# Fourier transform over tokens folded twice instead of once, the last attention combination on four piece buffers, and one weight load moved ahead in the dilated attention's queue

## The chip, the cores and the metric

One core of a Trainium2 chip runs one program. The metric is the device time of that program in microseconds (us); a shorter time is better. All arithmetic is in float32.

## The reference, cut to what matters

Two blocks run one after the other on 2048 tokens of width 1024. The change touches only the second. From its normalised input it projects a part `u_f` (512 wide) for a Fourier mixer, gates, and queries, keys and values for dilated window attention with three dilations, whose outputs are combined with softmax weights `alpha`.

```python
u_f = u_f.reshape(B, S, N_FOURIER_GROUPS, HEAD_DIM)
f = jnp.fft.fft2(u_f, axes=(1, 3), norm="ortho").real.astype(jnp.float32)
f = jnp.einsum('bsgc,gcd->bsgd', f, w_fourier.astype(jnp.float32)).reshape(B, S, FOURIER_WIDTH)
y_f = f * jax.nn.silu(g_f)
...
alpha = jax.nn.softmax(jnp.stack(lses, axis=0), axis=0)
o = jnp.sum(alpha[..., None] * jnp.stack(outs, axis=0), axis=0).reshape(B, S, ATTN_WIDTH)
y_a = o * jax.nn.silu(g_a)
mixed = jnp.concatenate([y_f, y_a], axis=-1) @ w_out.astype(jnp.float32)
h = h + mixed
```

The Fourier part runs over the 2048 tokens (the axis of the change) and over 64 channels of a group. Both are done as matrix products with tables of cosines and sines.

## The kernel before

The program is a row of blocks; in each, every engine has its own list of instructions, and they wait for each other on semaphores. At a block's end all engines meet. Matrix products on TensorE (PE) take four passes' worth of time per column in float32 and appear in the trace as two instructions (two passes over the columns) each.

**Dilated attention** (`dilated_attention`). Four groups g of 128 channels; in each, five steps n project two column blocks of the weights with seven products in place of eight (`SevenProducts`, `project`). A step needs four quarters of weights in `raw` (loads 0 to 3, `SevenProducts.load`, issued by SyncE, SP) and four differences `mixed` made by GpSimd (POOL, `SevenProducts.make`, L2353 to L2362). Product 2 of a step needs the second difference (L2356), which needs quarter 3. From g = 1 on, the step n = 5g also combines the attention outputs of group g - 1: the tokens are cut into eight pieces of 256; for each, SP fetches two stored outputs, the gate and the broadcast weights `alpha` (`fetch_piece`, L2511, L2512, L2519), POOL does five operations (`combine`, L2571 to L2578), and SP stores the result (`keep_piece`, L2529). A piece's fetch waits until the piece two before is combined, since there are two piece buffers.

**The Fourier block** (`fourier`). The combination of the last group is done here, beside the Fourier projections. The projections are ND = 2 rounds d of four units f (f = 4d to 4d + 3), seven products each (L3612) in the order 1, 2, 4, 6, 5, 7, 3; `HALVES` says which half of the tokens a unit takes. Units 4d and 4d + 1 make `us[0]` and `us[1]` (two channel groups of u), units 4d + 2 and 4d + 3 make their gates in `mix`. Products rotate over four PSUM banks; ScalarE (ACT) holds products 1 and 4 (`hold`, into `x` and `y`), VectorE (DVE) adds the others (`add`, L3768), POOL does two joins (`join`, L3554, L3557). The gates of round 0 lie in rows 2 and 3 of `mix_f`, where the two piece buffers are too, so `add` and `join` of unit 2 wait for all eight combined pieces (L3551, L3766).

After each round come two transforms over tokens, g = 2d and 2d + 1. DVE folds token t with token 2048 - t (`fold`, L3779 to L3783) into sums and differences of 1024 each; PE multiplies these by 128 x 128 channel matrices (L3638, 16 products of 128 columns), ACT copies the results to `co` (L3701), PE treats the middle token apart (L3643, L3646, L3647, L3656) and does 16 products of 512 columns with the table `trig` (L3654), of which 4 MB is fetched anew for each transform. ACT collects two of four result banks (`collect`, L3325), DVE joins them to 2048 tokens (`join`, L3335 to L3345) and multiplies by the gate (L3791).

**The output projection** (`project_second`) follows, 224 products at L2205. The last transform's join and gate product are done in it, and it needs four weight combinations that DVE makes (`FourierTail.make`, L3313 to L3318) from `w_out`.

Of the kernel before, what the change touches and what calls it, by code (L numbers as in the profile page):

```python
# [2077 lines left out]
def project_second(nc, t, mix_f, mix_att, hT, w, late, tail):  # L2078
# [6 lines left out]
    with ExitStack() as ctx:  # L2085
# [26 lines left out]
        def bank_of(j, i):  # L2112
            return (5 + ORDER.index((j, i))) % 8

        with nc.Block() as block:
# [99 lines left out]
            @block.scalar  # L2215
            def _(act):
                tail.collect(nc, act, bank, PAIRS - 1)
                for j in range(NJ):
                    act.wait_ge(prod, done(j, 1))
                    need(act, held, 7 * (j - 4) + 4)  # L2220
                    nc.scalar.copy(m1[:, j % 4], bank[bank_of(j, 1)][:]).then_inc(m1_out, 1)

            @block.vector
            def _(dve):
# [24 lines left out]
                tail.join(nc, dve, bank, PAIRS - 1)  # L2249
# [35 lines left out]
class SevenProducts:  # L2285
# [61 lines left out]
    def make(self, nc, pool, n):  # L2347
# [8 lines left out]
        nc.gpsimd.tensor_tensor(mixed[:, 1], raw[:, 3], mixed[:, 0], ALU.subtract).then_inc(self.made, 1)  # L2356
        need(pool, self.prod, done + 5)
# [96 lines left out]
class Combine:  # L2454
# [6 lines left out]
    def __init__(self, nc, ctx, sems):  # L2461
# [4 lines left out]
        piece = [self.rows[:, 2 + i, 0:6 * self.NQ].rearrange("p (m n) -> p m n", n=self.NQ) for i in range(2)]  # L2466
        self.alpha = [p[:, 0:3] for p in piece]
        self.others = [p[:, 3:5] for p in piece]
        self.gate = [p[:, 5] for p in piece]
# [11 lines left out]
        self.piece_in = [sem("c_piece_in0"), sem("c_piece_in1")]  # L2481
        self.weighed = sem("c_weighed")
# [4 lines left out]
        self.wo_in = [sem(f"c_wo{k}") for k in range(KC)]  # L2487

# [16 lines left out]
    def fetch_rows(self, sp, t, g, m):  # L2505

        NQ, i = self.NQ, m % 2
        cols = slice(m * NQ, (m + 1) * NQ)
        if m >= 2:
            sp.wait_ge(self.mixed, self.PIECES * g + m - 1)  # L2510
        sp.dma_start(self.others[i], t["o_rows"][g].rearrange("c p n -> p c n")[:, :, cols]).then_inc(self.piece_in[i], 16)  # L2511
        sp.dma_start(self.gate[i], t["g_rows"][g][:, cols]).then_inc(self.piece_in[i], 16)  # L2512

    def fetch_alpha(self, sp, t, g, m):

        half, NQ, i = P // 2, self.NQ, m % 2
        for h in range(2):
            rows = slice(h * half, (h + 1) * half)
            sp.dma_start(self.alpha[i][rows], t["alpha"][g, :, h, m * NQ:(m + 1) * NQ].partition_broadcast(half)).then_inc(self.piece_in[i], 16)  # L2519
# [44 lines left out]
    def combine(self, nc, pool, g, m, dst=None):  # L2564

        i = m % 2
        n = self.PIECES * g + m
        alpha, others, gate = self.alpha[i], self.others[i], self.gate[i]
        own = self.o[:, m * self.NQ:(m + 1) * self.NQ]
        pool.wait_ge(self.piece_in[i], 64 * (n // 2 + 1))  # L2570
# [10 lines left out]
def dilated_attention(nc, t, seven, late):  # L2581
# [33 lines left out]
    with ExitStack() as ctx:  # L2615
# [64 lines left out]
        with nc.Block() as block:  # L2680
            @block.sync
            def _(sp):
# [54 lines left out]
                for g in range(PAIRS):  # L2737
# [8 lines left out]
                    else:  # L2746
# [57 lines left out]
            def _(pool):  # L2804
# [12 lines left out]
                seven.make(nc, pool, 0)  # L2817
# [7 lines left out]
                for n in range(5 * PAIRS):  # L2825
                    g, p = divmod(n, 5)
                    mixing = g > 0 and p < 2
                    for j in range(2):
# [9 lines left out]
                        if mixing and p == 0:  # L2838
                            if j == 0:
                                late.weights_pool(nc, pool, g - 1)  # L2840
                            else:
                                pool.wait_ge(out, NB * N_CFG * g)
                                late.combine(nc, pool, g - 1, 0)
                                late.combine(nc, pool, g - 1, 1)
# [6 lines left out]
                    seven.make(nc, pool, n + 1)  # L2851
# [431 lines left out]
class FourierTail:  # L3283
# [4 lines left out]
    def __init__(self, nc, ctx, hT, room, sems):  # L3288
# [4 lines left out]
        self.ue = room[:, 5].rearrange("p (i n) -> p i n", i=2)  # L3293
        self.s = self.ue[:, :, :].rearrange("p i n -> p (i n)").rearrange("p (s n) -> p s n", n=M // 2)
        self.qs = sb("qs5", [P, 2, M // 2])
        self.mid_out = sb("mid_out5", [P, 1])
# [23 lines left out]
    def collect(self, nc, act, bank, g):  # L3320
# [3 lines left out]
        for i in range(2):  # L3324
            nc.scalar.copy(self.qs[:, i], bank[2 * i + 1][:]).then_inc(self.qs_out, 1)  # L3325
        nc.scalar.copy(self.mid_out[:], bank[4][:, 0:1]).then_inc(self.qs_out, 1)

    def join(self, nc, dve, bank, g):
# [3 lines left out]
        f, s, qs, mid_out, joined = self.us[g % 2], self.s, self.qs, self.mid_out, self.joined  # L3332
        dve.wait_ge(self.qs_out, 3 * g + 3)
        for i in range(2):
            nc.vector.tensor_tensor(s[:, 2 * i], bank[2 * i][:], qs[:, i], ALU.add).then_inc(joined, 1)  # L3335
# [591 lines left out]
```

## Time and profile before

| | us |
|---|---|
| time, median of 3 runs (3505.53 to 3507.4) | 3505.95 |
| time of the profiled execution | 3506.91 |
| span of the profile (first to last instruction) | 3504.9 |
| PE busy | 3353.2 (96%) |
| DVE, ACT, POOL busy | 1284.6, 1017.1, 918.6 |
| mean granted TensorE clock | 0.986 |

The span is the time from the first to the last instruction in the profile; what the run's time has beyond it (2.0 us here) lies around the program. The profiled execution is 0.96 us above the median. In the rows below, "x8" of a PE line counts instructions, two to a product; the number before a line's engine is its duration, the one before that its start, both in us.

### The profile page before, as it was taken

What the parts mean: (1) busy time and instruction counts of PE and PEld (TensorE: products, weight loads), DVE (VectorE), ACT (ScalarE), POOL (GpSimd) and SP (SyncE); (2) the same over time, 40 slices, a digit from 0 to 9 for tenths busy, and PEclk for the clock granted to TensorE, in tenths of its full rate; (3) what the DMA queues carried; (4) which work ended last, traced back from release to release, by engine and by line L of the source; (5) the groups of instructions that cost most, each with busy time, mean ns of one, the idle gap of its engine ahead of it and who ended that gap; (6) DMA issues with size and microseconds to landing.
All of it is one profiled execution on the core that took longest, in us unless ns stands there. A gap on an engine that the chain in (4) does not pass through costs nothing. (4 is left out here: it accounts for less than half of the span.)

```text
span 3504.9 us, 43834 instructions
## 1 busy us (share of the span) xinstructions
PE 3353.2 (96%) x16395; PEld 1818.3 (52%) x16395; DVE 1284.6 (37%) x2780; ACT 1017.1 (29%) x2411; POOL 918.6 (26%) x705
## 2 busy tenths in 40 slices
PE   8999999998999999998999999999999999889999
PEld 4485858583545445443544554445454545444444
DVE  3344352534424434444323432333243324423422
ACT  4313131331414323332323422442243224110100
POOL 1002020206253352534211241124112321421132
PEclk9999999999999999999999999999999999999999
DMA  7101010113021123221167154725372726331421
GB/s 229 28 20 36 20 37 13 32 59 84 17 51 28 37 46 134 90 96 48 31 34 49 44 90 37 49 56 75 40 46 58 75 44 38 87 117 53 192 96 60
DMA packets 284381, 217.11 MB, mean 62 GB/s; under 512 B 124604, under 2 KB 249932, under 8 KB 278752
## 3 DMA queue, kind: packets, MB, share of 16 engines
q1 hardware_dynamic: 281068, 214.30, 31.4%
q8 instruction: 132, 2.16, 0.3%
q14 instruction: 77, 0.63, 0.1%
q10 hardware_dynamic: 3104, 0.01, 0.1%
HBM read 168.47 MB, written 45.81 MB: 61 GB/s over the span
## 5 line engine op out<-in xcount | busy, mean ns | idle before, releaser
L2406 PE MATMUL d<-hT,w_tiles 128*128 128x512 f32 x1280 | 579.4, 596 | 5.2 <-DMA w_tiles<-in_w_in 5.2
L2406 PE MATMUL d<-w_room,w_tiles 128*128 128x512 f32 x960 | 440.8, 602 | 17.3 <-POOL w_tiles L2356 17.3
L2406 PEld LDWEIGHTS d<-hT,w_tiles 128*128 128x128 f32 x1280 | 242.4, 191 | 303.9 <-issue 296.8
L549 PE MATMUL m<-hT,w 128*128 128x512 f32 x704 | 321.1, 593 | 1.3 <-ACT pre L699 1.3
L2406 PEld LDWEIGHTS d<-w_room,w_tiles 128*128 128x128 f32 x960 | 182.8, 193 | 243.4 <-issue 220.9
L2443 POOL TENSOR_TENSOR w_z<-w_u,w_y 128x512 f32<-128x512 f32 x40 | 50.7, 1268 | 814.5 <-ACT w_y L2412 814.5
L1364 PE MATMUL n<-hT,wo 128*128 128x512 f32 x512 | 226.5, 597 | 4.8 <-DMA wo<-in_w_in 4.8
L549 PEld LDWEIGHTS m<-hT,w 128*128 128x128 f32 x704 | 124.9, 191 | 116.0 <-issue 115.8
L1364 PE MATMUL n<-mix_na,wo 128*128 128x512 f32 x384 | 169.4, 594 | 0.9 <-POOL wo L1264 0.9
L3056 ACT ACTIVATE mix_f<-sneg,negmax 128x192 f32<-128x192 f32 (+1 forms) x384 | 161.0, 426 | 5.6 <-DVE negmax L3170 5.6
L1364 PEld LDWEIGHTS n<-hT,wo 128*128 128x128 f32 x512 | 96.7, 191 | 125.6 <-issue 120.0
L497 POOL TENSOR_TENSOR hn<-hn 128x512 f32<-128x512 f32 x16 | 17.5, 1094 | 544.3 <-DVE hn L866 544.3
L563 PEld LDWEIGHTS m<-w,hT 128*128 128x128 f32 x1280 | 143.6, 192 | 2.4 <-issue 1.4
L563 PE MATMUL m<-w,hT 128*128 128x128 f32 x1280 | 143.9, 275 | 0.8 <-DVE v L815 0.8
L3612 PE MATMUL f<-hT,w_tiles 128*128 128x512 f32 x256 | 115.4, 607 | 13.0 <-DVE mix_f L3768 8.8
L1364 PEld LDWEIGHTS n<-mix_na,wo 128*128 128x128 f32 x384 | 71.7, 190 | 87.7 <-issue 85.3
L3170 DVE CUSTOM_DVE_ANT_0 sneg<-d,bias 128x192 f32<-128x192 f32 (+1 forms) x384 | 108.3, 324 | 23.4 <-PE d L2901 14.6
L2867 PE MATMUL d<-sq,ones 128*128 128x512 f32 x192 | 98.8, 596 | 4.2 <-ACT sq L3022 4.2
L2435 DVE TENSOR_TENSOR w_u<-d,w_u 128x512 f32<-128x512 f32 x64 | 44.3, 692 | 147.7 <-PE d L2406 147.7
L3027 ACT ACTIVATE rt<-d,eps 128x512 f32<-128x512 f32 x96 | 66.0, 688 | 108.2 <-PE d L2867 108.2
L2915 PE MATMUL d<-ident,mix_f 128*128 128x128 f32 x600 | 85.9, 280 | 9.0 <-ACT mix_f L3056 7.5
L3612 PE MATMUL f<-w_room,w_tiles 128*128 128x512 f32 x192 | 85.8, 604 | 8.1 <-POOL w_tiles L3541 8.1
(389 smaller groups left out, 5230.3 us busy)
## 6 DMA issues: line engine op xcount, KB each, us to landing
w_tiles<-in_w_in SPq DMA_DIRECT2D x96, 256.0 KB, 3.1
trig<-in_trig SPq DMA_DIRECT2D x16, 1024.0 KB, 4.9
mix_f<-alpha SPq DMA_DIRECT2D x64, 192.0 KB, 6.4
ada<-in_w_ada SPq DMA_DIRECT2D x8, 1024.0 KB, 11.5
xg<-in_x SPq DMA_DIRECT2D x4, 2048.0 KB, 16.2
w<-in_w_in SPq DMA_DIRECT2D x16, 512.0 KB, 3.9
rb<-r_rows SPq DMA_DIRECT2D x16, 512.0 KB, 4.9
wo<-in_w_in SPq DMA_DIRECT2D x32, 256.0 KB, 3.4
```

The costliest lines, as they stand in the source:

```text
L549: last = nc.tensor.matmul(bank[n % 2][:], w[:, k], hT[:, k, (n % 4) * TB:(n % 4 + 1) * TB], start=(k == 0), stop=(k == KC - 1))
L563: last = nc.tensor.matmul(bank[n % 2][:, j * P:(j + 1) * P], hT[:, k, c * P:(c + 1) * P], w[:, k], start=(k == 0), stop=(k == KC - 1))
L1364: last = nc.tensor.matmul(bank_of(f, i)[:], w[:, k], xs[k], start=(k == 0), stop=(k == h - 1))
L2406: last = nc.tensor.matmul(bank[self.bank_of(n, j, i)][:], w[:, k], x[k], start=(k == 0), stop=(k == h - 1))
L2435: nc.vector.tensor_tensor(dst, bank[self.bank_of(n, j, i)][:], other, ALU.add).then_inc(self.full, 1)
L2443: nc.gpsimd.tensor_tensor(self.z[:], u, self.y[:], ALU.add).then_inc(self.pooled, 1)
L2867: nc.tensor.matmul(bank[S_BANK][:], ones[:], sq[:, e % 2], start=True, stop=True).then_inc(ssq, 1)
L2915: last = nc.tensor.transpose(bank[T_BANK + j][:, i * P:(i + 1) * P], prob[:, u % (2 * BU), part_ * P:(part_ + 1) * P], ident[:])
L3027: nc.scalar.activation(rt[:, e % 2], bank[S_BANK][:], ACT.Ln, bias=epst[:, 0:1], scale=1.0 / half).then_inc(rooted, 1)
L3056: nc.scalar.activation(prob[:, u % (2 * BU), off:off + n], sneg[:, (U * a + u) % 6, 0:n], ACT.Exp, bias=negmax[:, c, u:u + 1], scale=-1.0, ...
L3170: nc.vector.tensor_tensor_reduce(out=sneg[:, (U * a + u) % 6, 0:n], in0=bank[b][:, c0:c0 + n], in1=bias[:, i % 2, c, t0:t0 + n], scale=1.0 ...
L3612: last = nc.tensor.matmul(bank_of(f, i)[:], w[:, k], xs[k], start=(k == 0), stop=(k == h - 1))
```

## The change

Three things change.

- **Dilated attention**: SP issues load 3 of step 5g + 1 before piece 2 and not after it; `make` is cut in two, and POOL combines piece 1 between the halves and not before both.
- **Last combination**: its pieces use four buffers that lie in the memory of `trig` and `co` (not yet in use then). So SP can fetch four pieces at once, and `add` and `join` of unit 2 no longer wait for it. The softmax factors come earlier in the lists of DVE, ACT and POOL. The makes of the next weights are interleaved otherwise with the pieces.
- **Transform**: the tokens are folded twice. `fold` first adds and subtracts token t and t + 1024, then folds each half, in place in `us`; the table is a quarter in size (2 MB, fetched once, after the last combined piece). The 16 products with it have 256 columns. There are two sets of four banks, so the channel products of transform 2d + 1 are issued between the products of transform 2d, and the middle tokens of both in one go (`middles`). `fold(2d + 1)` moves before unit 4d + 3's adds, and `FourierTail.make` before `finish(2)`.

```diff
     def fetch_rows(self, sp, t, g, m):
-        NQ, i = self.NQ, m % 2
+        NQ = self.NQ
+        landed, _, others, gate = self.piece(g, m)
+        depth = 4 if g == PAIRS - 1 else 2
         cols = slice(m * NQ, (m + 1) * NQ)
-        if m >= 2:
-            sp.wait_ge(self.mixed, self.PIECES * g + m - 1)
+        if m >= depth:
+            sp.wait_ge(self.mixed, self.PIECES * g + m - depth + 1)
...
                         load(n + 1, 2)
                         fetch_bias(g)
+                        load(n + 1, 3)
                         late.fetch_piece(sp, t, g - 1, 2)
                         late.keep_piece(sp, t, g - 1, 0)
-                        load(n + 1, 3)
...
-                    seven.make(nc, pool, n + 1)
+                    seven.make_first(nc, pool, n + 1)
+                    if mixing and p == 0:
+                        late.combine(nc, pool, g - 1, 1)
+                    seven.make_last(nc, pool, n + 1)
...
-        trig = sb("trig5", [P, NTR, 4, H])
+        trig = sb("trig5", [P, NK, 4, 2, Q])
-        co = sb("co5", [P, 2, MC, P])
+        co = sb("co5", [P, 2, 4, 2, NK, P])
+        late.wide = [trig[:, i].rearrange("p n e j -> p (n e j)") for i in range(2)] + [co[:, e].rearrange("p s r k c -> p (s r k c)") for e in range(2)]
...
+                def fetch_trig(k):
+                    sp.wait_ge(late.mixed, late.PIECES * PAIRS)
+                    sp.dma_start(trig[:, k], t["trig"][k]).then_inc(trig_in, 16)
...
+                for m in range(2):
+                    late.fetch_piece(sp, t, LAST, m + 4)
+                    late.keep_piece(sp, t, LAST, m)
                 load(N0 + 1, 0)
+                late.fetch_piece(sp, t, LAST, 6)
+                late.keep_piece(sp, t, LAST, 2)
+                late.fetch_piece(sp, t, LAST, 7)
+                late.keep_piece(sp, t, LAST, 3)
                 load(N0 + 1, 3)
...
-                sp.wait_ge(prod, 7 * 4 * ND)
+                sp.wait_ge(prod, product_no(4 * ND - 1, 5))
+                for k in range(PAIRS, KC):
+                    fetch_out(k)
                 for k in range(PAIRS):
                     fetch_out(k)
...
-                        elif d == 0:
-                            pool.wait_ge(late.mixed, late.PIECES * PAIRS)
...
+                def coefficients(g):
...
+                    for i in range(2):
+                        pe.wait_ge(folded, 12 * g + 7 + 5 * i)
+                        for r in range(2):
+                            for m in range(4):
+                                c = 4 * (2 * i + r) + m
+                                last = nc.tensor.matmul(second_banks[2 * i + r][:, m * P:(m + 1) * P], us[e][:, c * P:(c + 1) * P], ab[:, e, i], start=True, stop=True)
+                        last.then_inc(coef, 1)
+                def middles(d):
+                    pe.wait_ge(full, 5 * 4 * (d + 1))
+                    pe.wait_ge(pooled, 2 * 4 * (d + 1))
+                    pe.wait_ge(folded, 12 * (2 * d + 1) + 12)
+                    for e in range(2):
+                        last = nc.tensor.matmul(first_banks[3][0:1, e * P:(e + 1) * P], us[e][:, M:M + 1], ab[:, e, 0], start=True, stop=True)
+                    last.then_inc(mids, 1)
+                def transform(g, n):
...
+                    for odd in range(2):
+                        for k in range(NK):
+                            stop = k == NK - 1 and not (n == 0 and odd == 0)
+                            last = nc.tensor.matmul(dst[:, odd * Q:(odd + 1) * Q], co[:, e, 2 * i + odd, r, k], trig[:, k, n, odd], start=(k == 0), stop=stop)
+                        if n == 0 and odd == 0:
+                            pe.wait_ge(mids_out, d + 1)
...
                 def fold(g):
...
+                    nc.vector.tensor_tensor(p, u[:, 0:M], u[:, M:T], ALU.add).then_inc(folded, 1)
+                    nc.vector.tensor_tensor(q, u[:, 0:M], u[:, M:T], ALU.subtract).then_inc(folded, 1)
+                    dve.wait_ge(folded, 12 * g + 2)
+                    for s0 in (0, 2):
+                        for s, src in ((s0, p), (s0 + 1, q)):
+                            op = ALU.add if s in (0, 3) else ALU.subtract
+                            nc.vector.tensor_tensor(part[:, s, 0, 1:Q], src[:, 2:H:2], src[:, M - 2:H:-2], op).then_inc(folded, 1)
+                            nc.vector.tensor_tensor(part[:, s, 1], src[:, 1:H:2], src[:, M - 1:H:-2], op).then_inc(folded, 1)
+                        nc.vector.tensor_copy(singles(s0), of_both(0 if s0 == 0 else H)).then_inc(folded, 1)
```

The first place is one transform on PE, the pair after round 0 (a row is a group of products; `f0` to `f7` are the PSUM banks, `mid5` the middle token's row). Before, it stands so:

```order
L3643 MATMUL f0<-ab5,w_room 1x128
L3646 MATMUL f0<-alt_row5,mid5 128x512
L3647 MATMUL f4<-one5,mid5 128x1
L3654 MATMUL f0<-trig5,co5 128x512
L3654 MATMUL f1<-trig5,co5 128x512
L3654 MATMUL f2<-trig5,co5 128x512
L3654 MATMUL f3<-trig5,co5 128x512
L3656 MATMUL f4<-alt_col,co5 128x1
```

Of the change, the same place and what follows up to transform 1's first bank:

```order
L3658 MATMUL f3<-ab5,w_room 1x128 x2
L3674 MATMUL f0<-trig5,co5 128x256 x2
L3677 MATMUL f0<-alt_row5,mid5 128x256
L3674 MATMUL f0<-trig5,co5 128x256 x2
L3674 MATMUL f1<-trig5,co5 128x256 x4
L3687 MATMUL f3<-alt_col,co5 128x1 x2
L3688 MATMUL f3<-one5,mid5 128x1
L3649 MATMUL f4<-ab5,w_room 128x128 x4
L3649 MATMUL f5<-ab5,w_room 128x128 x4
L3649 MATMUL f6<-ab5,w_room 128x128 x4
L3649 MATMUL f7<-ab5,w_room 128x128 x4
L3674 MATMUL f2<-trig5,co5 128x256 x4
```

The table products went from 512 to 256 columns at the same number, the middle row's product came behind two of them, and the next transform's channel products (L3649) stand in the middle.

The second place is SP's queue in the dilated attention, g = 1, from the bias fetch on (`w_tiles` is the weight quarter, the rest are pieces). Before:

```order
L2693 DMA bias<-in_alibi 64x576 x2
L2511 DMA mix_f<-o_rows 128x2x256
L2512 DMA mix_f<-g_rows 128x256
L2519 DMA mix_f<-alpha 64x3x256 x2
L2529 DMA att_rows<-mix_f 128x256
L2345 DMA w_tiles<-in_w_in 128x4x128
```

And of the change:

```order
L2708 DMA bias<-in_alibi 64x576 x2
L2345 DMA w_tiles<-in_w_in 128x4x128
L2526 DMA mix_f<-o_rows 128x2x256
L2527 DMA mix_f<-g_rows 128x256
L2535 DMA mix_f<-alpha 64x3x256 x2
L2545 DMA att_rows<-mix_f 128x256
```

The quarter moved past a fetch that waits for piece 0 and a store that does too.

The third place is POOL in the Fourier block, from the third combined piece to the fifth (`L2586` is the first of a piece's five operations, `L3565` and `L3568` the joins of a unit, `L3554` a weight difference). Of the change:

```order
L2593 TENSOR_TENSOR mix_f<-mix_f,co 128x256
L3565 TENSOR_TENSOR w_room<-u,qs 128x512
L2586 TENSOR_TENSOR co<-co 128x512
L2587 TENSOR_TENSOR mix_f<-mix_f,co 128x256
L2589 TENSOR_TENSOR mix_f<-mix_f,co 128x256
L2591 TENSOR_TENSOR mix_f<-mix_f,co 128x256
L2593 TENSOR_TENSOR mix_f<-mix_f,co 128x256
L3554 TENSOR_TENSOR w_tiles<-w_tiles 128x512
L3568 TENSOR_TENSOR w_room<-u,qs 128x512
L2586 TENSOR_TENSOR trig<-trig 128x512
```

Pieces lie in `co` and `trig` in place of `mix_f`, and the first weight difference stands ahead of the join and not behind it; all eight pieces still stand ahead of unit 2's first join.

## Rows read from the trace of the kernel before

**Rows 1.** Whom PE waited for: us in total, times, longest.

```profile
PE d L2406 <- POOL w_tiles L2356: 17.3, 4, 5.7
PE f L3612 <- DVE mix_f L3768: 8.8, 1, 8.8
PE f L3612 <- POOL w_tiles L3541: 8.1, 1, 8.1
PE f L3612 <- DVE w_room L3768: 3.0, 1, 3.0
```

**Rows 2.** Timeline of PE, dilated attention: a product undisturbed, then three after a wait.

```profile
2003.61 3.60 PE L2406 MATMUL d<-w_room,w_tiles 128*128 128x512 f32 x8
2021.62 6.01 PE L2406 MATMUL d<-w_room,w_tiles 128*128 128x512 f32 x8 [4.97 <-POOL w_tiles L2356]
2365.63 6.38 PE L2406 MATMUL d<-w_room,w_tiles 128*128 128x512 f32 x8 [5.74 <-POOL w_tiles L2356]
2709.25 5.24 PE L2406 MATMUL d<-w_room,w_tiles 128*128 128x512 f32 x8 [5.02 <-POOL w_tiles L2356]
```

**Rows 3.** Timeline of SP and POOL at the first of these places.

```profile
2013.21 0.39 SPq L2345 DMA_DIRECT2D w_tiles<-in_w_in  x1
2020.30 1.26 POOL L2356 TENSOR_TENSOR w_tiles<-w_tiles 128x512 f32<-128x512 f32 x1 [2.74 <-DMA w_tiles<-in_w_in]
2010.20 2.17 POOL L2571 TENSOR_TENSOR mix_f<-mix_f 128x512 f32<-128x512 f32 x1
```

**Rows 4.** Timeline of PE: ends of rounds 0 and 1, the output's start.

```profile
2990.91 3.67 PE L3612 MATMUL f<-hT,w_tiles 128*128 128x512 f32 x8 [1.23 <-PEq L76]
3103.55 10.46 PE L3612 MATMUL f<-hT,w_tiles 128*128 128x512 f32 x24
3162.16 3.68 PE L3612 MATMUL f<-hT,w_tiles 128*128 128x512 f32 x8
3248.97 10.46 PE L3612 MATMUL f<-hT,w_tiles 128*128 128x512 f32 x24
3307.11 10.54 PE L2205 MATMUL f<-hT,w_room 128*128 128x512 f32 x24 [1.14 <-PEq L76]
```

**Rows 5.** Timeline of SP and POOL in round 0.

```profile
3011.45 1.28 SPq L2502 DMA_DIRECT2D alpha<-part  x3
3002.22 2.68 POOL L3554 TENSOR_TENSOR w_room<-u,qs 128x512 f32<-128x512 f32 x1 [11.01 <-ACT qs L3684]
3020.84 1.27 POOL L2571 TENSOR_TENSOR mix_f<-mix_f 128x512 f32<-128x512 f32 x1 [9.41 <-DMA mix_f<-alpha]
3025.16 1.26 POOL L2571 TENSOR_TENSOR mix_f<-mix_f 128x512 f32<-128x512 f32 x1
3086.09 1.26 POOL L3554 TENSOR_TENSOR mix_f<-u,qs 128x512 f32<-128x512 f32 x1 [0.17 <-POOL mix_f L2578]
```

**Rows 6.** DMA issues from 3033 to 3046 us: KB each, median us to landing.

```profile
w_tiles<-in_w_in SPq DMA_DIRECT2D x2, 256.0 KB, 8.5
```

**Rows 7.** Timeline of PE in the first transform.

```profile
3114.79 3.84 PE L3638 MATMUL f<-ab,w_room 128*128 128x128 f32 x32 [0.78 <-DVE mix_f L3768]
3126.33 0.28 PE L3656 MATMUL f<-alt_col,co 128*128 128x1 f32 x2
3126.47 3.68 PE L3654 MATMUL f<-trig,co 128*128 128x512 f32 x8
3129.99 0.28 PE L3656 MATMUL f<-alt_col,co 128*128 128x1 f32 x2
```

**Rows 8.** Timeline of PE in the first block: a product of 258 columns and its successor.

```profile
453.39 0.60 PE L605 MATMUL m<-state,qT 128*128 128x258 f32 x2
453.85 0.71 PE L611 MATMUL m<-v,sd 128*128 128x129 f32 x4
```

**Rows 9.** Timeline of DVE: a join's first operation and its gate product.

```profile
3163.51 0.69 DVE L3335 TENSOR_TENSOR w_room<-f,qs 128x512 f32<-128x512 f32 x1 [14.61 <-ACT mid_out L3326]
3168.81 2.29 DVE L3791 TENSOR_TENSOR mix_f<-w_room,mix_f 128x2048 f32<-128x2048 f32 x1
```

More of the change, by code:

```diff
@@ L2465, in __init__ @@
         self.o = self.rows[:, 1]
[L2466 to L2469, printed above, removed]
+        self.near = [self.rows[:, 2 + i] for i in range(2)]
+        self.wide = None
         self.stat = sb("stat6", [P, 2, N_CFG, U])
@@ L3463, in _ @@
                 late.fetch_stats(sp, t, LAST)
-                late.fetch_rows(sp, t, LAST, 0)
-                late.fetch_rows(sp, t, LAST, 1)
+                for m in range(4):
+                    late.fetch_rows(sp, t, LAST, m)
+                load(N0 + 1, 1)
+                late.store_alpha(sp, t, LAST)
+                for m in range(4):
+                    late.fetch_alpha(sp, t, LAST, m)
                 sp.wait_ge(once, 2)
@@ L3568, in _ @@
                 late.combine(nc, pool, LAST, 3)
+                make(N0 + 1, 1)
                 join(1, 2)
[L3570 removed]
                 late.combine(nc, pool, LAST, 4)
[L3572 to L3574 removed]
+                make(N0 + 1, 2)
+                make(N0 + 1, 3)
+                late.combine(nc, pool, LAST, 5)
+                make(N0 + 1, 4)
+                for m in range(6, late.PIECES):
                     late.combine(nc, pool, LAST, m)
@@ L3617, in weigh_channels @@
                         pe.wait_ge(consts, 48)
+                    else:
+                        pe.wait_ge(joined, 12 * (2 * d - 1) + 4)
                     pe.wait_ge(wd_in, 64 * (d + 1))
-                    need(pe, qs_out, 3 * 2 * d)
                     for e in range(2):
                         for i in range(2):
-                            last = nc.tensor.matmul(bank[3][:, (2 * e + i) * P:(2 * e + i + 1) * P], chan[:, i], wd[:, e], start=True, stop=True)
+                            last = nc.tensor.matmul(second_banks[3][:, (2 * e + i) * P:(2 * e + i + 1) * P], chan[:, i], wd[:, e], start=True, stop=True)
@@ L3633, in transform @@
                     for i in range(2):
-                        pe.wait_ge(folded, 6 * g + 4 + 2 * i)
-                        for m in range(MC):
-                            if e == 1 and i == 1 and m == 4:
-                                pe.wait_ge(qs_out, 3 * g)
-                            last = nc.tensor.matmul(bank[BANKS[2 * i + m // 4]][:, (m % 4) * P:(m % 4 + 1) * P], ue[:, i, m * P:(m + 1) * P], ab[:, e, i], start=True, stop=True)
-                        last.then_inc(coef, 1)
-                    if g > 0:
-                        pe.wait_ge(qs_out, 3 * g)
-                        pe.wait_ge(joined, 12 * (g - 1) + 4)
@@ new lines, in transform @@
+                def transform(g, n):
+                    d, e = divmod(g, 2)
+                    i, r = divmod(n, 2)
+                    dst = tail.banks(g)[n]
+                    pe.wait_ge(co_out, 4 * g + 2 + 2 * i)
+                    if g == 0 and n == 0:
+                        pe.wait_ge(trig_in, 16 * NK)
+                    if n == 3:
+                        pe.wait_ge(centre_out, g + 1)
+                    for odd in range(2):
+                        for k in range(NK):
+                            stop = k == NK - 1 and not (n == 0 and odd == 0)
+                            last = nc.tensor.matmul(dst[:, odd * Q:(odd + 1) * Q], co[:, e, 2 * i + odd, r, k], trig[:, k, n, odd], start=(k == 0), stop=stop)
+                        if n == 0 and odd == 0:
+                            pe.wait_ge(mids_out, d + 1)
+                            nc.tensor.matmul(dst[:, 0:Q].rearrange("p (n c) -> p n c", c=P), mid[0:1, e], alt_row[:, :].unsqueeze(1).broadcast_to([1, Q // P, P]), start=False, stop=True)
+                    if n == 3:
+                        last.then_inc(done, 1)
@@ L3659, in _, with output_centre @@
+                def output_centre(g):
+                    d, e = divmod(g, 2)
+                    dst = tail.banks(g)[3][:, H - 1:H]
+                    pe.wait_ge(co_out, 4 * g + 4)
+                    for k in range(NK):
+                        nc.tensor.matmul(dst, co[:, e, 0, 0, k], alt_col[:], start=(k == 0), stop=False)
+                    nc.tensor.matmul(dst, mid[0:1, e], one[0:1, :], start=False, stop=True).then_inc(centre, 1)
                 for d in range(ND):
```

265 lines of the change are left out of this document (119 added, 146 removed).

## The prediction

> **What bounds the kernel now.** I read the shares of busy time first: TensorE (PE) works 96% of the span, so time is won only where PE has less to do or stops waiting. So I asked next whom PE waits for [rows 1]. Four entries touch this change: 17.3 us for the weight difference of L2356 in the dilated attention, and 8.8, 8.1 and 3.0 us in the Fourier block. Then the timeline of PE at each. In the dilated attention there are three long waits, one in each of the groups 1 to 3: 4.97, 5.74 and 5.02 us, 15.73 together (the fourth of the 17.3 is at the stage's start and stays). The same rows show a second loss: the eight passes behind a wait take 6.01, 6.38 and 5.24 us, where 3.60 is the undisturbed figure [rows 2], 6.83 us more in all. PE's clock is at its lower level (1.2 GHz, half of 2.4) behind such a stop.
>
> In the Fourier block, rounds 0 and 1 are the same work on PE. Round 0 runs from 2990.91 to 3114.01 (3103.55 + 10.46), 123.10 us; round 1 from 3162.16 to 3259.43, 97.27 us [rows 4]. So round 0 loses 25.83 us; 19.9 of it are the three waits [rows 1], 5.9 the clock behind them. The transforms take 48.15 us after round 0 (3114.01 to 3162.16) and 47.68 us after round 1 (3259.43 to 3307.11, change of block included) [rows 4]. I work with these four stretches.
>
> **Part 1, the weight quarter in the dilated attention.** POOL starts L2356 at 2020.30, released by the DMA of quarter 3, which SP issued at 2013.21 [rows 3] behind a fetch and a store that wait for the first piece. The load's own condition is product 6 of the half step before, whose passes start at 2003.61 [rows 2] and are over at about 2007.1. So it goes out 6 us earlier, and no piece's transfers are ahead of it. POOL now makes the two differences before piece 1, which starts at 2010.20 today [rows 3]. If the quarter still takes 7.1 us to land (2013.21 to 2020.30), the second difference is done at 2015.5; if POOL's list sets it, at 2012.8. PE wants it at 2016.65 (2021.62 less its wait). Cover 1.1 to 3.8 us; I take the whole 15.73 + 6.83 = 22.6 us.
>
> What is late next: piece 1 and the last two differences now stand between PE's earlier start and the next unit's first join. At 4.32 us a piece (3020.84 to 3025.16, [rows 5]) and one wait for a fetch, that join comes some 4 us after its input. It holds up the addition of product 5, whose bank PE wants back three products later; over 6 us are left. I leave 1 us of loss: **-21.6 us**. Bounds: 17 (the quarter late by 1 us each time, with part of the clock loss) to 22.6.
>
> **Part 2, round 0.** POOL's list is the clock here. Today the first join starts at 3002.22, `alpha` goes out at 3011.45, the first piece is combined from 3020.84, and unit 2's first join starts at 3086.09, behind all eight pieces [rows 5]; PE's 8.8 us wait is for the addition behind it. In the changed order the factors no longer wait for the first join but for DVE's three sums (over at about 2997.8), so I put store and first piece 6 us earlier: 3014.8. From there eight pieces are 34.6 us, two joins and four differences of 1.2 to 1.3 us are 7.5: 3056.9 with no wait. Two things are added.
> - Quarter 3 of the next weights goes out behind piece 3 and the fetch of piece 7, at about 3036.5. Loads in this stretch took 8.5 us to land [rows 6]; I take 7.5, so the second difference is made at about 3046.7. PE, if it never stops, wants it for its sixteenth product: 15 at 3.44 us (97.27 less 0.9 for the channel weights, by 28 products) and that 0.9 are 3043.4. **A wait of 3.3 us, and 1.7 us of clock behind it**, a little under a third of 6.83.
> - An operation of DVE on two tensors in SBUF holds POOL up: 2.68 us beside one [rows 5] for what takes 1.26 alone [rows 3]. Fold 0 and two changes of sums fall into POOL's pieces: 3 to 6 us.
>
> So unit 2's join is done at 3063 to 3067. With the stop above, PE wants its bank at about 3069; without it at 3064. No second stop, then. Of 25.8 us, 5.0 stay: **-20.8 us**. Bounds: no stop (-25.8), and 12 us (-13.8: the difference 5 us late, the join 3 us, each with 2 us of clock).
>
> The Trainium skill (SBUF — State Buffer, "Who interferes with whom") says that VectorE and GpSimd hold their shared port pair as an exclusive lock. The trace agrees in kind (2.68 against 1.26 us). By the rule fold 0 (some 5 us) and both changes (2.3 us each) would be POOL's loss in full, and the join would be done at about 3068.
>
> **Part 3, the transforms.** Per transform the channel products stay, 32 passes of 128 columns in 3.8 us. The table products stay 16 in number, 32 passes; eight of 512 columns take 3.52 us (3126.47 to 3129.99), 0.44 each [rows 7]. A pass of 256 columns doesn't stand in the trace; the nearest has 258, two in 0.46 us (453.39 to 453.85, [rows 8]), weight loads among them, and 0.22 is half of 0.44. Between 0.22 and 0.23 I take 0.22: 7.0 us (14.1 before). The middle row's product is 0.44, the centre column three products of 0.14 (3126.33 to 3126.47, [rows 7]), the middle token 0.24. A transform is 3.8 + 7.04 + 0.44 + 0.42 + 0.24 = 11.94 us, two are 23.9. Waits: the middle row is wanted some 5.1 us in, and ACT is through with four copies and the row some 5.4 us in: 0.3 us. Today's waits go: 0.78 us at the start [rows 7], since the channel products don't wait for the last addition, and those for the join of the transform before, since the two have banks of their own. Pair 0: 24.2 in place of 48.15, **-24.0 us**.
>
> Pair 1 ends with a change of block, where all engines meet, and there DVE sets the end. Transform 2 is done 16.2 us into the pair, ACT has copied two banks by 17.5, join and gate product take 7.6 us (3163.51 to 3168.81 + 2.29, [rows 9]): 25.1, and 1.14 us for the change of block [rows 4]: 26.3 in place of 47.68, **-21.4 us**. `FourierTail.make`, four operations of 2.29 us, stands ahead of this join. `w_out` is asked for two products (6.9 us) before the pair begins; if it is there 8 us into it, `make` is done in time, and what is later goes to the end one for one. I allow 2 us.
>
> Folding costs DVE more, some 5 us in place of 2.8 by the columns, and fold 1 or 3 runs ahead of the last unit's additions. DVE is free for 6 us there (one more product's time less an addition), and behind it PE has three more banks, 10 us: nothing. The join now writes every second column; I price that as today, at the worst 1.5 us more.
>
> **Sum.** -21.6 - 20.8 - 24.0 - 21.4 = -87.8. The profiled execution took 3506.91, so 3419.1; the median lies 0.96 below it: **3418 us**.
>
> **Rivals.**
> 1. *The four terms hold*, with 0 to 8 us lost in round 0 (chance 0.70): 3411 to 3424.
> 2. *Round 0's stall moves instead of going* (0.14). POOL still has all eight pieces ahead of unit 2's join, and four pieces of `alpha` share the queues with the weight quarter. For it: the 8.5 us landing; against it: 2 to 6 us of cover for the join. With 9 us or more of stops: 3423 to 3432.
> 3. *The shorter passes don't take half* (0.07). If something other than the columns set a pass's time (its weight load, say) and it stayed at 0.44, 128 passes would cost 28 us more: 3446; half of that loss is 3432. Against it: the two passes of 258 columns, which have loads too. The Trainium skill (TensorE: Matmul & The Clock Gate, "The mechanism") says that loads overlap running matmuls only in another row group; by it this would be the case. The measured 0.46 us doesn't agree.
> 4. *No stop in round 0 and DVE off the end* (0.06): 3408 to 3411.
> 5. *The change doesn't do what it says* (0.02): the load isn't what PE waits for, and the rounds' waits reappear; it would need three terms to fail.
> 6. *Slower than before* (0.01): PE's clock stays at the lower level through the short passes. That costs as much again as the work done under it; both pairs are 48 us, and it decides from 88 us of work on, so it would have to last 40 us into the rounds. Against it: the clock came back inside eight passes after each stop [rows 2].
>
> **Range.** 3408 to 3434. Down: 5.0 (no stop), 1.0 (part 1's rest), 1.1 (DVE off the end), 2 to 3 for the spread of runs and of my starts. Up: 7 (12 us of stops), 4.6 (part 1 at its low bound), 3.4 (one fall of the clock in each pair), 1. About 0.2% (7 us) is what a measurement of this kernel can tell from no change. Faster by more than that 0.97, within it 0.02, slower 0.01.
>
> **What the profile after would show.** Part 1: no wait of PE over 1 us for the second difference in groups 1 to 3, and the next join later behind its input. Part 2: round 0 of 97 to 105 us, one wait of some 3 us at product 2 of unit 2, for POOL's weight difference, and none for DVE's addition in unit 2. Part 3: passes of 256 columns 0.22 us apart, pairs of about 24 and 26 us, PE's last block released by DVE's gate product. The prediction is wrong if PE waits over 5 us at unit 3's first products, if the passes are 0.3 us or more apart, or if `w_out` holds up the end.

## The result, and the profile after

The median went from 3505.74 us (3505.16 to 3507.4, 4 runs) to **3426.16 us** (3422.98 to 3429.14, 4 runs): ratio 0.9771, 95% interval [0.9756, 0.9786]. The prediction was 3418 (3408 to 3434). The profiled execution took 3427.26 us with a span of 3425.4, against 3506.91 and 3504.9: 79.65 us less where the sum had 87.8. Each term can be read off TensorE's (PE's) timeline. Here are the starts that answer to [rows 4]:

```profile
2977.63 3.67 PE L3622 MATMUL f<-hT,w_tiles 128*128 128x512 f32 x8 [1.24 <-PEq L76]
...
3032.84 12.26 PE L3622 MATMUL f<-w_room,w_tiles 128*128 128x512 f32 x24 [2.58 <-POOL w_tiles L3554]
...
3068.98 10.46 PE L3622 MATMUL f<-hT,w_tiles 128*128 128x512 f32 x24
3079.28 3.73 PE L3649 MATMUL f<-ab,w_room 128*128 128x128 f32 x32
...
3092.26 4.48 PE L3674 MATMUL f<-trig,co 128*128 128x256 f32 x20
...
3104.29 1.02 PE L3622 MATMUL f<-hT,w_tiles 128*128 128x512 f32 x2
...
3199.60 1.88 PE L3622 MATMUL f<-hT,w_tiles 128*128 128x512 f32 x4
...
3227.59 2.81 PE L2205 MATMUL f<-hT,w_room 128*128 128x512 f32 x6 [1.10 <-PEq L76]
```

A row is start, duration, instruction, and in brackets how long PE had stood still and for whom. Taking each stretch from these starts, and that of before from [rows 4]:

| stretch | before | after | difference | forecast |
|---|---|---|---|---|
| all ahead of the Fourier block | 2990.91 | 2977.63 | -13.3 | -21.6 |
| round 0 | 123.10 | 101.81 | -21.3 | -20.8 |
| transforms, pair 0 | 48.15 | 24.85 | -23.3 | -24.0 |
| round 1 | 97.27 | 97.19 | -0.1 | 0 |
| transforms, pair 1, with the change of block | 47.68 | 26.11 | -21.6 | -21.4 |

Round 0 ends at 3068.98 + 10.46 = 3079.44, round 1 at 3199.60 + 1.88 = 3201.48. Three terms are right to 0.7 us, and the first is short by 8.3, about what the sum as a whole is short by (8.15). Of its 13.3 us, 1.15 lie ahead of the first scores of the dilated attention (1929.63 before, 1928.48 after), in code that is the same in both; from there to the Fourier block it is 12.1. Yet the waits that it counted are gone. What PE waited for after (whom, us in total, times, longest), with one entry of ScalarE (ACT) that the kernel before doesn't have:

```profile
PE d L2919 <- issue: 12.8, 8, 3.4
PE d L2412 <- DMA w_tiles<-in_w_in: 5.3, 1, 5.3
PE d L2412 <- POOL w_tiles L2357: 2.6, 1, 2.6
ACT w_y L2418 <- DMA v_rows<-w_y: 42.9, 3, 14.9
```

Of the four waits for the second weight difference in [rows 1] only that at the stage's start is left. At the place of [rows 3] the quarter now leaves at 2006.12, the difference is made at 2011.31 with no wait, and PE's product starts at 2015.32. But the first line, PE's scores, was 7.2 us with a longest of 0.9 before. The new stop is at the end of the value projections of groups 1 to 3. Timeline after: the load and the difference just named, PE, then the engines behind the new stop in the order in which they release each other:

```profile
2006.12 0.38 SPq L2345 DMA_DIRECT2D w_tiles<-in_w_in  x1
2011.31 1.27 POOL L2357 TENSOR_TENSOR w_tiles<-w_tiles 128x512 f32<-128x512 f32 x1
2015.32 3.60 PE L2412 MATMUL d<-w_room,w_tiles 128*128 128x512 f32 x8
...
2056.52 3.60 PE L2412 MATMUL d<-hT,w_tiles 128*128 128x512 f32 x8
2063.49 1.15 PE L2919 MATMUL d<-kT,mix_f 64*64 64x128 f32 x16 [3.37 <-issue]
2064.56 1.98 PE L2900 MATMUL d<-ident,pt 128*128 128x128 f32 x8
...
2402.80 1.56 PE L2919 MATMUL d<-kT,mix_f 64*64 64x128 f32 x16 [3.09 <-issue]
...
2741.90 0.88 PE L2919 MATMUL d<-kT,mix_f 64*64 64x128 f32 x16 [1.88 <-issue]
...
2044.18 0.38 SPq L2526 DMA_DIRECT2D mix_f<-o_rows  x1
2047.51 0.43 SPq L2740 DMA_DIRECT2D v_rows<-w_y  x1
...
2055.10 0.59 ACT L2418 COPY w_y<-d 128x512 f32<-128x512 f32 x1 [14.91 <-DMA v_rows<-w_y]
2055.86 1.27 POOL L2449 TENSOR_TENSOR w_z<-w_u,w_y 128x512 f32<-128x512 f32 x1 [4.99 <-DMA v_rows<-w_z]
2057.16 0.69 DVE L2441 TENSOR_TENSOR w_u<-d,w_u 128x512 f32<-128x512 f32 x1 [9.98 <-POOL w_z L2449]
2057.08 1.27 POOL L2586 TENSOR_TENSOR mix_f<-mix_f 128x512 f32<-128x512 f32 x1
2061.40 1.26 POOL L2452 TENSOR_TENSOR w_y<-w_u,w_y 128x512 f32<-128x512 f32 x1
2062.69 0.69 DVE L2441 TENSOR_TENSOR pt<-d,w_u 128x512 f32<-128x512 f32 x1 [4.25 <-POOL w_y L2452]
```

SyncE (SP) fetches piece 7 at 2044.18, when piece 5 is combined, and issues the store of the first value block (`w_y`, `w_z`) only behind that, at 2047.51. The store, behind the piece's transfers, takes 7.6 us to land. ACT needs `w_y` for the next half step and copies into it at 2055.10. GpSimd's (POOL's) join and VectorE's (DVE's) addition follow. Then POOL combines piece 7, 4.3 us that stand between its two joins in the kernel before as well; its second join starts at 2061.40, and DVE's last addition is over at 2063.38. The scores start 0.1 us later. In the kernel before the same places read:

```profile
2049.46 1.19 SPq L2725 DMA_DIRECT2D v_rows<-w_y  x1
...
2058.63 0.59 ACT L2412 COPY w_y<-d 128x512 f32<-128x512 f32 x1 [9.71 <-PE d L2406]
...
2069.73 0.88 PE L2901 MATMUL d<-kT,mix_f 64*64 64x128 f32 x16 [0.90 <-issue]
```

There the store left at 2049.46 and ACT came for `w_y` 9.2 us later, released by PE. After the change PE is 8.7 us further at this place (its last projection ends at 2060.12 in place of 2068.84), but the store is only 1.95 us earlier, because the pieces keep their own pace. ACT would have come for `w_y` 8.7 us earlier too, at 2049.9, and gets it at 2055.10, 5.2 us late. Of these, 2.5 us reach PE as the longer stop (3.37 for 0.90); the scores and transposes behind it then run partly at the lower clock (1.98 for eight transposes that take 1.24 undisturbed, section 2; the granted clock is 0.58 from 2063.49 to 2066.50, and 0.50 behind the stop at 2402.80).

### The profile page after: what moved, and what is told of

It reads as the page before. It is cut to its first block and busy times, and to the rows that moved or that the text cites. A ratio compares the mean times of both kernels' runs of the same rounds, so it can differ in the third digit from the quotient of the medians.

```text
span 3425.4 us, 43810 instructions
## 1 busy us (share of the span) xinstructions
PE 3307.9 (97%) x16379; PEld 1812.2 (53%) x16379; DVE 1299.9 (38%) x2804; ACT 1016.2 (30%) x2409; POOL 923.5 (27%) x705
## 5 line engine op out<-in xcount | busy, mean ns | idle before, releaser
L2919 PE MATMUL d<-kT,mix_f 64*64 64x192 f32 (+1 forms) x1536 | 80.2, 319 | 17.7 <-issue 12.8
## 6 DMA issues: line engine op xcount, KB each, us to landing
ada<-in_w_ada SPq DMA_DIRECT2D x8, 1024.0 KB, 11.6
```

Of the source, the lines that this page charges most:

```text
L2919: last = nc.tensor.matmul(bank[b][dst, c0:c0 + n], q[src, u * half:(u + 1) * half], kT[src, k0:k0 + n], start=True, stop=True)
```

## The experiments

All ratios are to runs of the kernel before on the same chip.

### 1. Each part alone

The dilated part alone in the kernel before is the diff's load, `make_first` and `make_last`, nothing of the Fourier block. The Fourier part alone is the kernel after with these lines undone:

```diff
                         fetch_bias(g)
-                        load(n + 1, 3)
                         late.fetch_piece(sp, t, g - 1, 2)
                         late.keep_piece(sp, t, g - 1, 0)
+                        load(n + 1, 3)
...
                                 late.combine(nc, pool, g - 1, 0)
+                                late.combine(nc, pool, g - 1, 1)
...
                     seven.make_first(nc, pool, n + 1)
-                    if mixing and p == 0:
-                        late.combine(nc, pool, g - 1, 1)
                     seven.make_last(nc, pool, n + 1)
```

> The kernel before with the dilated part alone (the quarter's load ahead of piece 2 and the weight differences split around piece 1). The sum of the prediction, with nothing late behind the stop: -21.6 us, so 3484 us against 3505.7. Theory A (the stop moves: the store of the first value block leaves SyncE's queue too late, ScalarE's copy into w_y waits for it, and the scores start 2.5, 2.2 and 1.0 us later, with 1.4 to 2.5 us of clock behind each): -12 us, 3493.7 us, and in the trace ScalarE waits for v_rows<-w_y by some 40 us in all as in the kernel after. Rival B (the shortfall is made by the two parts together, not by this one): 3484 us and no such waits.

> The kernel after with the dilated part undone. The two parts share no engine time, so by the prediction's terms -20.8 - 24.0 - 21.4 = -66.2 us, 3439.5 us; by the trace of after (-21.3, -23.3, -21.6) 3439.5 us too. If the missing 8 us came from the Fourier block, it would be 3447 us.

Measured: 3493.23 us for the dilated part, ratio 0.9964 [0.9951, 0.9976], and 3439.9 us for the Fourier part, 0.9812 [0.9798, 0.9825]. Both medians are within 0.5 us of what was expected, the first of them by theory A; that run's five times spread over 10 us (3487.94 to 3497.84), so that close an agreement is partly luck, but theory A's 12 and rival B's 21.6 us are well apart. The dilated part alone leaves the same wait of ACT and the same stop behind it:

```profile
ACT w_y L2418 <- DMA v_rows<-w_y: 44.6, 3, 15.0
PE d L2910 <- issue: 14.4, 8, 3.5
```

So the shortfall belongs to the dilated part by itself, and the parts add up: -12.3 and -65.7 are -78.0, against -79.6 for both.

### 2. The store ahead of piece 7

```diff
                         late.keep_piece(sp, t, g - 1, 4)
+                        store_block(n + 1, 0, t["v_rows"][g])
                         late.fetch_piece(sp, t, g - 1, 7)
                         late.keep_piece(sp, t, g - 1, 5)
-                        store_block(n + 1, 0, t["v_rows"][g])
```

It was made on the kernel after, on the kernel before with the dilated part, and on the kernel before by itself.

> The kernel after with the stores of the first value block issued ahead of the fetch of piece 7 instead of behind it. Theory A: ScalarE's copy into w_y waits for no store, the scores start 0.9 us behind the last projection again, and 5.6 us of stops and 4 to 5 us of clock go: 3415 to 3417 us. Rival C (what makes the scores late is VectorPool work itself, GpSimd's joins standing behind the pieces, whose pace is set by their fetches of 6.4 us each): no change, 3426 us, the same stops of 3.4 us, and ScalarE's copy no earlier to any use.

> The kernel before with the dilated part and the first value block's stores ahead of piece 7. Theory A (the store alone stood between the dilated part and its full worth): 3484 us, the -21.6 us of the prediction's first term, with no wait of ScalarE for v_rows<-w_y. Rival (some of the 21.6 was never there): the -12.3 of the part alone less the 9.9 that the store brought in the whole kernel gives no less than 3483, so anything above 3487 would speak for it.

> The kernel before with nothing but the first value block's stores ahead of piece 7. ScalarE's copy waited for no store there, so by theory A nothing changes: 3506 us, within 2. Rival (the early store is worth 10 us by itself, whatever the dilated part does): 3496 us.

Measured, in this order: 3416.25 us (0.9745 [0.9731, 0.9758]); 3484.48 us (0.9937 [0.9924, 0.9949]); 3506.27 us (0.9997 [0.9988, 1.0005]). In the kernel after the moved store leaves at 2039.77, ACT waits for PE alone, and the stop is gone with the slow passes behind it:

```profile
2039.77 0.43 SPq L2740 DMA_DIRECT2D v_rows<-w_y  x1
...
2049.12 0.58 ACT L2418 COPY w_y<-d 128x512 f32<-128x512 f32 x1 [9.71 <-PE d L2412]
...
2060.23 0.88 PE L2919 MATMUL d<-kT,mix_f 64*64 64x128 f32 x16 [0.90 <-issue]
2061.04 1.24 PE L2900 MATMUL d<-ident,pt 128*128 128x128 f32 x8
```

The three together settle it. The same edit is worth 9.9 us behind the dilated part and nothing before it, and the dilated part with it is worth 3505.7 - 3484.5 = 21.2 us (to 3507.53, the median of its own chip, 23.1), where the forecast had 21.6. The traces say it more sharply. From the first scores of group 0 to the Fourier block it is 1061.28 us before, 1049.15 after, and 1038.14 and 1038.17 in the two kernels with the dilated part and the early store: 23.1 us less than before, 11.0 less than after. (In the second of the two, PE's wait for a weight difference in round 0 is 10.3 us where it was 8.1, which is what its whole time has less.) Rival C (POOL's joins behind the pieces) falls: POOL's order of work is the same here, piece 7 between the joins included, and the stop is gone.

### 3. Half the dilated part

One run moves the load and leaves all four differences behind piece 1, another splits the differences and leaves the load.

> The kernel after without the split of the weight differences: the quarter's load is ahead of piece 2, but piece 1 is combined ahead of all four differences. GpSimd's piece of 4.33 us then stands in front of the second difference, which ended at 2012.6 in the kernel after and would end at 2016.9, against a product that wants it at about 2015.5 in its trace: a stop of 1 to 2 us and 1.5 us of clock, three times, while the late store and the stop ahead of the scores stay: 3432 to 3436 us. Rival: the load alone did it, and the split is worth nothing: 3426 us.

> The kernel after with the quarter's load where it was, behind the store of piece 0, and the differences split around piece 1. The load leaves at about 2012 and lands 7 us later, as in the kernel before, and GpSimd now waits for it with piece 1 behind it: a stop of some 5 us as in the kernel before stays, three times, and the pieces come later too, so that the stop ahead of the scores grows: 3450 us or more, up to that of the Fourier part alone (3440) plus 15. Rival: the split alone is enough: 3426 us.

Measured: 3427.04 us (0.9773 [0.976, 0.9787]) without the split, 3439.56 us (0.9807 [0.9794, 0.9821]) without the load. Both expectations were too high, for one reason. The first number is that of the rival (the split is worth nothing), but not for its reason, that PE would not stop. Without the split PE does stop for the second difference, as expected, but the stop at the scores is then gone:

```profile
2017.73 5.40 PE L2412 MATMUL d<-w_room,w_tiles 128*128 128x512 f32 x8 [2.36 <-POOL w_tiles L2357]
...
2065.22 0.88 PE L2918 MATMUL d<-kT,mix_f 64*64 64x128 f32 x16 [0.90 <-issue]
```

PE loses 2.36 us and 1.80 of clock (5.40 for 3.60) at the first place, and no longer arrives too early at the second. In groups 2 and 3 it stops as long, but the passes behind take 3.70 us: the same stop costs the clock in one group and not in the others. I had added the two stops; they take each other's place, and with the late store the split is worth nothing that can be told. Without the load ahead the stops for the difference are 4.62, 5.25 and 4.38 us, one longer stop at the scores is left (2.09, group 2), and the time is that of the Fourier part alone. If that is so, the split must be worth something once the store is early, which the last run of the next section tests.

### 4. Round 0: its one stop, and the one behind it

The stop of 2.58 us was in the forecast: POOL has the second difference at 3031.52, since quarter 3 leaves SP at 3024.84. The next kernel (with the early store) issues quarter 0 one piece earlier and quarter 3 two (not one, as the expectation below has it), and makes the second difference ahead of piece 4. The one after it also puts unit 2's first join ahead of piece 7:

```diff
-                for m in range(2):
-                    late.fetch_piece(sp, t, LAST, m + 4)
-                    late.keep_piece(sp, t, LAST, m)
+                late.fetch_piece(sp, t, LAST, 4)
+                late.keep_piece(sp, t, LAST, 0)
                 load(N0 + 1, 0)
+                late.fetch_piece(sp, t, LAST, 5)
+                late.keep_piece(sp, t, LAST, 1)
+                load(N0 + 1, 3)
                 late.fetch_piece(sp, t, LAST, 6)
                 late.keep_piece(sp, t, LAST, 2)
                 late.fetch_piece(sp, t, LAST, 7)
                 late.keep_piece(sp, t, LAST, 3)
-                load(N0 + 1, 3)
...
                 join(1, 2)
+                make(N0 + 1, 2)
                 late.combine(nc, pool, LAST, 4)
-                make(N0 + 1, 2)
...
                 make(N0 + 1, 4)
-                for m in range(6, late.PIECES):
-                    late.combine(nc, pool, LAST, m)
+                late.combine(nc, pool, LAST, 6)
+                join(2, 1)
+                late.combine(nc, pool, LAST, 7)
                 for f in range(2, 4 * ND):
-                    join(f, 1)
+                    if f > 2:
+                        join(f, 1)
```

> The kernel of the store moved ahead, and in the first round of the Fourier block the loads of weight quarters 0 and 3 one fetched piece earlier each, with the second weight difference ahead of the fifth combined piece. TensorE's only stop of that round (2.58 us, for the second difference, and 1.8 us of clock behind it) should go: 4.4 us below the run of the store alone, 3411 to 3413 us. Rival: the joined rows of unit 2, which stand behind the pieces on GpSimd and were done at 75 us of the round, become the stop, and the gain is under 2 us.

> The kernel of the run before (store and quarters ahead), with the first join of unit 2 in the Fourier block ahead of the last combined piece on GpSimd. There the stop had only moved: TensorE waited 2.76 us for VectorE's addition to unit 2's rows, which stood behind GpSimd's join at 3039.28. Theory D (the join stands behind the pieces, and is ready to run after the seventh): the join runs 4.3 us earlier, the round has no stop and no fall of the clock, and 4.4 us go: 3410 us (3409 to 3411). Rival: VectorE's own fold in front of that addition sets it, and the time stays at 3414.

Measured: 3414.44 us (0.9738 [0.9725, 0.9751]) and then 3411.45 us (0.9731 [0.9718, 0.9745]). In the first of them the rival won. PE's stop for the weight difference is gone, and the join, still behind all eight pieces, takes its place:

```profile
3041.39 5.27 PE L3623 MATMUL f<-hT,w_tiles 128*128 128x512 f32 x8 [2.76 <-DVE mix_f L3820]
...
3038.60 0.72 POOL L2593 TENSOR_TENSOR mix_f<-mix_f,co 128x256 f32<-128x256 f32 x1
3039.28 1.26 POOL L3566 TENSOR_TENSOR mix_f<-u,qs 128x512 f32<-128x512 f32 x1
```

Round 0 takes 101.70 us there (2965.40 to 3067.10). With the join ahead of piece 7 no wait is left in it:

```profile
2965.52 3.67 PE L3625 MATMUL f<-hT,w_tiles 128*128 128x512 f32 x8 [1.24 <-PEq L76]
...
3062.62 3.73 PE L3652 MATMUL f<-ab,w_room 128*128 128x128 f32 x32
```

That is 97.10 us, 4.6 less, as theory D has it. The medians differ by 3.0 us only, and the intervals overlap, so the size of this last step rests on the trace.

Then the split is undone in this fastest kernel, as in section 3:

> The kernel of the join ahead of the last piece (3411.5 us), with all four weight differences behind piece 1 again. Theory E (the split's worth was hidden in the kernel after by the late store, and shows once the store is early): three stops of some 2 us for the second difference and 1.8 us of clock each come back and nothing later makes them up: 3421 us (3419 to 3424). Rival (the split is worth nothing in itself): 3411.5 us.

Measured: 3421.88 us, 0.9758 [0.9745, 0.9771]. Behind an early store the split is worth 10.4 us (9.5 by the ratios), behind the late one 0.9, which is nothing that can be told. Theory E holds, and PE's waits for the second difference are back, four of 9.9 us together where the kernel with the split has one of 2.8; in group 2 the passes behind take 5.40 us, in groups 1 and 3 3.70.

### 5. Two piece buffers in the last combination

The kernel after with a depth of 2 for the last combination, and its fetches and loads in the order of before:

```diff
-        i = m % (4 if last else 2)
+        i = m % 2
...
-        depth = 4 if g == PAIRS - 1 else 2
+        depth = 2
```

> The kernel after with two piece buffers in the last combination, the fetches in the order of before. By the rows of before, unit 2's join stood 65.3 us behind the first piece (3020.84 to 3086.09), against 51.4 us with four buffers. If the wait for the fetches makes that difference, the join comes at about 24.0 + 65.3 = 89.3 us of the round and TensorE stops some 14 us for it: 3438 to 3444 us. Rival (GpSimd's own work of 4.33 us a piece is the pace, and the earlier store of alpha did all): within 2 us of 3426.

Measured: 3431.59 us, 0.9787 [0.9774, 0.98], between the two expectations, and outside both. The fetches hold POOL up at two pieces, by 5.57 us (piece 2 starts 9.92 us behind piece 1) and by 1.49 us (piece 4), but PE waits once, and not for the join:

```profile
3005.08 1.26 POOL L2586 TENSOR_TENSOR trig<-trig 128x512 f32<-128x512 f32 x1
3015.00 1.27 POOL L2586 TENSOR_TENSOR trig<-trig 128x512 f32<-128x512 f32 x1 [5.57 <-DMA trig<-alpha]
...
3053.10 1.26 POOL L2586 TENSOR_TENSOR trig<-trig 128x512 f32<-128x512 f32 x1
3057.40 1.26 POOL L3566 TENSOR_TENSOR mix_f<-u,qs 128x512 f32<-128x512 f32 x1
...
3036.25 13.35 PE L3623 MATMUL f<-w_room,w_tiles 128*128 128x512 f32 x24 [7.62 <-POOL w_tiles L3555]
3083.76 3.73 PE L3650 MATMUL f<-ab,w_room 128*128 128x128 f32 x32
```

Piece 7 starts at 3053.10 and the join at 3057.40, 81.4 us into the round that begins at 2975.99, not 89. From the first piece (3000.77) to the join it is 56.6 us, with four buffers 51.4, before 65.3. The stop for the weight difference had already put PE back far enough for the join. Round 0 takes 107.77 us against 101.81. Four buffers, with the order of fetches and loads that goes with them, are worth 6 us of the 21.3; what the rest of that term owes to the earlier `alpha` and to the order on the other engines was not taken apart.

## Why the prediction was right, and what it missed

The time was 3426 where the sum had 3418: inside the range, just above rival 1's 3411 to 3424. It lies in rival 2's 3423 to 3432, but that rival's mechanism (9 us or more of stops in round 0) did not happen. Three of the four terms held. Part 1 gave little more than half of its size (12.1 us of 21.6); that the time was inside the range all the same is owed to the room kept for the other terms.

- **Part 1, its direct half.** Right. The waits for the second difference are gone, and the passes behind them take 3.60 us. The second difference is done at 2012.58, set by POOL's list as in the forecast's 2012.8, and no load holds it up. With the store out of the way (section 2) that stretch gains 23.1 us, against the 22.6 of the direct half.
- **Part 1, "what is late next".** Here is the step that failed: "I leave 1 us of loss". It cost 9.9 us by the medians of the runs with and without the early store, 11.0 in their traces. I followed POOL's list from piece 1 to the unit's first join, and did not ask SP's queue the same question. SP's order ties the store of the value block to the fetch of piece 7, which waits for piece 5. The low bound of 17 us was derived from a late quarter only, and did not cover it. My own sentence named "the next join later behind its input"; the wait appeared one half step further on, through a buffer (`w_y`) and not through a join.
- **Part 2.** Right in size and, for PE, in mechanism: 101.81 us (forecast 97.3 + 5.0), one wait of 2.58 us (3.3) at the place named and for the weight difference, 1.80 us of clock (12.26 for 10.46; forecast 1.7), none for DVE. (The prediction calls 1.7 a little under a third of 6.83; it is a quarter, a third would be 2.3.) The first piece came 24.0 us into the round (forecast 23.9). Unit 2's join started at 75.4 us and was done at 76.6, where the forecast had 72.1 to 76.1 for its end. Its own terms don't reach that far: 3056.9, 3 to 6 for DVE and 1.3 for the join itself give 3061 to 3064, not 3063 to 3067. In the trace POOL loses 6.6 us beside DVE (2.5 in fold 0, 4.1 beside the two changes of sums) and waits 2.6 us for two weight quarters, which the sum left out. That without the stop PE wants the join's bank at 3064, 73.1 us into the round, was right: take the stop away and PE waits from 73.2 us (3041.39 less 2.76, less 2965.40), for 2.76 us (section 4). So the low bound and rival 4, both with no stop in round 0, were not to be had by removing the one stop; by the forecast's own 3063 to 3067 for the join they were already doubtful. POOL's first piece and unit 2's join in the kernel after:

```profile
3001.63 1.27 POOL L2586 TENSOR_TENSOR trig<-trig 128x512 f32<-128x512 f32 x1 [4.46 <-DMA trig<-alpha]
...
3052.98 1.26 POOL L3565 TENSOR_TENSOR mix_f<-u,qs 128x512 f32<-128x512 f32 x1
```

- **Part 3.** Twenty passes of 256 columns take 4.48 us, 0.22 each; rival 3 is out. Pair 0 has no wait at all and took 24.85 (24.2), with the middle row at 0.62 a product where I had 0.44, and the centre column and the middle token a little more than forecast. Pair 1 took 26.11 (26.3), with DVE's gate product done 0.9 us before PE's next product:

```profile
3208.85 2.29 DVE L3331 TENSOR_TENSOR hT<-hT 128x2048 f32<-128x2048 f32 x1 [6.64 <-DMA hT<-in_w_out]
...
3219.06 2.48 DVE L3359 TENSOR_TENSOR w_room<-f,qs 128x512 f32<-128x512 f32 x4 [1.19 <-ACT qs L3346]
...
3224.37 2.29 DVE L3845 TENSOR_TENSOR mix_f<-w_room,mix_f 128x2048 f32<-128x2048 f32 x1
```

`w_out` was there 7.4 us into the pair, and `make` was done 1.2 us before ACT was: the 2 us that I allowed were not needed. The join's strided writes cost nothing visible, four operations in 2.48 us.

The fastest kernel, with the store, the quarters and the join moved, takes 3411.45 us, 14.7 less than the change as made.

## What to carry to other kernels

When a stall of an engine goes away, list everything that a slower, untouched chain releases for it later, on the DMA-issuing queue too: a buffer's store that stands behind another chain's fetch has a slack that shrinks by what was won. Two stops fed by one such chain need not add: here taking the first away showed the second, and an edit that seemed to do nothing (the split, 0.9 us) was worth 10.4 behind the next fix. So test an edit again once its neighbour is mended.

## What the hardware showed that I had not expected

I had counted only what POOL loses beside DVE; in fold 0 DVE lost more. Fold 0 ran beside the pieces in 11.6 us, fold 1 alone in 5.2. The two stretches (us, then busy time of PE, its weight loads (PEld), DVE, ACT and POOL, then the granted clock, the share of the DMA engines and GB/s):

```profile
3026.70:3038.30 11.60, 9.02 (x24) 4.34 (x23) 11.56 (x13) 1.17 (x2) 10.69 (x10) 0.85 0.37 91
3059.15:3064.40 5.25, 5.25 (x14) 2.38 (x13) 5.22 (x14) 2.14 (x4) 0.05 (x1) 1.00 0.59 204
```

POOL's operations that start in the first stretch take 8.2 us where they are undisturbed (1.26 or 1.27 for 512 columns, 0.73 for 256) and took 10.7. One behind the other, both engines' work would be 5.2 + 8.2 = 13.4 us, and it took 11.6. The Trainium skill (SBUF — State Buffer, "Who interferes with whom") calls the shared ports an exclusive lock; the trace agrees that each is held up by the other, but shows some 2 us of overlap. Most of the loss was on DVE's side (6.4 us), and PE never waited for it.
